# Long and short products in turn, with an accumulator of their own for the short ones

## The reference, cut to what matters

```python
x = x + rms_norm(concat(mixers(h @ w_in)) @ w_out)                      # first block
gate, val = split(conv(h @ ffn_up)); x = x + rms_norm((gelu(gate) * val) @ ffn_down)
x = x + 0.5 * (silu(h @ ffn1_w_gate) * (h @ ffn1_w_up)) @ ffn1_w_down # second block
y = attention(h @ w_in_2); x = x + gated(y @ w_dil_branch, y @ w_diff_branch) @ w_out_2
x = x + 0.5 * (silu(h @ ffn2_w_gate) * (h @ ffn2_w_up)) @ ffn2_w_down
```

## Time and profile before

| | |
|---|---|
| median of 3 runs | 3406.97 us (3406.35 to 3409.04) |
| the profiled execution | 3409.16 us |
| its span | 3407.3 us |
| TensorE matmuls busy | 3380.9 us, 99% |
| TensorE weight loads busy | 2953.4 us, 87% |
| VectorE / ScalarE / GpSimd busy | 2250.2 / 1746.8 / 541.1 us |
| DMA | 616.16 MB, 181 GB/s |

### The profile page before, as it was taken

One profiled execution on the slowest core, in us unless ns is written; L12 is line 12 of the kernel. 1 busy time (PEld: TensorE's weight loads), 2 busy tenths in 40 slices (PEclk: granted clock), 3 DMA queues, 4 the chain that ended last, 5 costly groups with the idle time before them and its releaser, 6 DMA issues.

```text
span 3407.3 us, 59138 instructions
## 1 busy us (share of the span) xinstructions
PE 3380.9 (99%) x19590; PEld 2953.4 (87%) x19590; DVE 2250.2 (66%) x2934; ACT 1746.8 (51%) x2591; POOL 541.1 (16%) x508
## 2 busy tenths in 40 slices
PE   9999999999999999999999999999999999999999
PEld 7898888888888888888888888888888888888888
DVE  7868687777754475555555599856687656556544
ACT  5445565555544455445444455544566544444433
POOL 1204111111100011111100056611100111111000
PEclk9999999999999999999999999999999999999999
DMA  6524545555566645555566655554556555555665
GB/s 210 161 94 147 189 152 185 190 190 186 188 187 190 189 157 187 185 191 189 186 184 191 215 173 177 181 167 157 171 192 196 188 188 186 187 192 186 185 192 171
DMA packets 175601, 616.16 MB, mean 181 GB/s; under 512 B 20864, under 2 KB 21408, under 8 KB 175136
## 3 DMA queue, kind: packets, MB, share of 16 engines
q1 hardware_dynamic: 175088, 609.84, 55.7%
q10 hardware_dynamic: 432, 5.24, 0.4%
HBM read 610.81 MB, written 4.19 MB: 180 GB/s over the span
## 4 chain that ended last, share of the span: by engine, by line
PE 95%; DVE 2%; issue 1%; ACT 1%; DMA 0%; POOL 0%; DVEq 0%; SPq 0%; POOLq 0%; ACTq 0%
PE acc L393 60%; PE acc L396 30%; DVE weights_low L279 1%; PE acc L408 1%; PE ps_scale L603 1%; PE ps_narrow L2297 0%; PE ps_wide L2273 0%; ACT weights_high L272 0%; PE acc L411 0%; DVE halves_memory L494 0%; PE ps_wide L1380 0%; PE ps_wide L1426 0%; PE ps_wide L1390 0%; PE ps_wide L1384 0%; DMA weights_raw<-in_w_diff_branch 0%
## 5 line engine op out<-in xcount | busy, mean ns | idle before, releaser
L393 PE MATMUL acc<-moving_halves,weights_high 128*128 128x512 f32 x6400 | 2039.6, 399 | 1.8 <-DVE x_T L2566 1.8
L279 DVE TENSOR_TENSOR weights_low<-weights_raw,weights_high 128x1024 fp32r<-128x1024 f32 (+2 forms) x1184 | 1450.0, 1237 | 738.0 <-ACT weights_high L272 736.7
L272 ACT ACTIVATE weights_high<-weights_raw 128x1024 fp32r<-128x1024 f32 (+2 forms) x1184 | 1220.6, 1032 | 797.5 <-PE acc L396 771.6
L396 PEld LDWEIGHTS acc<-moving_halves,weights_low 128*128 128x128 f32 x6400 | 1204.1, 188 | 284.2
L396 PE MATMUL acc<-moving_halves,weights_low 128*128 128x256 f32 x6400 | 1259.3, 278 | 0.0
L393 PEld LDWEIGHTS acc<-moving_halves,weights_high 128*128 128x128 f32 x6400 | 980.3, 189 | 13.3 <-issue 9.8
L393 PE MATMUL acc<-gated_halves,weights_high 128*128 128x512 f32 x2024 | 635.6, 395 | 0.0
L488 ACT ACTIVATE cross_products<-acc 128x256 f32<-128x256 f32 x509 | 194.6, 382 | 693.8 <-PE acc L396 693.7
L396 PEld LDWEIGHTS acc<-gated_halves,weights_low 128*128 128x128 f32 x2024 | 380.2, 188 | 89.9
L511 POOL TENSOR_TENSOR stage_scratch<-unscaled,token_scale 128x256 f32<-128x256 f32 x264 | 217.9, 826 | 1302.6 <-DVE unscaled L494 778.2
L396 PE MATMUL acc<-gated_halves,weights_low 128*128 128x256 f32 x2024 | 397.6, 278 | 0.0
(11 more groups left out here) (361 smaller groups left out, 1972.3 us busy)
## 6 DMA issues: line engine op xcount, KB each, us to landing
weights_raw<-in_w_in SPq DMA_DIRECT2D x271, 512.0 KB, 4.0
weights_raw<-in_ffn_up SPq DMA_DIRECT2D x176, 512.0 KB, 4.3
weights_raw<-in_ffn_w_gate SPq DMA_DIRECT2D x176, 512.0 KB, 4.1
weights_raw<-in_ffn_w_up SPq DMA_DIRECT2D x176, 512.0 KB, 4.6
weights_raw<-in_ffn_w_down SPq DMA_DIRECT2D x160, 512.0 KB, 3.9
weights_raw<-in_ffn_down SPq DMA_DIRECT2D x80, 512.0 KB, 4.2
weights_raw<-in_w_out SPq DMA_DIRECT2D x64, 512.0 KB, 3.8
weights_raw<-in_ffn_w_down SPq DMA_DIRECT2D x32, 256.0 KB, 2.7
```

The lines of the kernel that those rows point to most:

```text
L272: core.nc.scalar.activation(core.high[:, slot, k0:nk, :].rearrange("p a b -> p (a b)"), core.raw[:, slot, k0 * P:nk * P], ACT.Copy).then_i ...
L279: core.nc.vector.tensor_tensor(core.low[:, slot, k0:nk, :].rearrange("p a b -> p (a b)"), core.raw[:, slot, k0 * P:nk * P], core.high[:, s ...
L393: core.nc.tensor.matmul(acc[:, t % 2, :, :], core.high[:, u % SLOTS, k, :], parts[:, prod.first[t] + k0 + k, :, :], start=(k0 + k == 0), s ...
L396: core.last = core.nc.tensor.matmul(acc[:, t % 2, 0, :], core.low[:, u % SLOTS, k, :], parts[:, prod.first[t] + k0 + k, 0, :], start=False ...
```

## The change

A product can be marked with `place_apart`. Its short products then go to a second accumulator, the two banks of the first `ps_wide` tensor, and long and short matmuls are issued in turn: long, short, long, short. The take gets one more operation on VectorE: the short products' sum is added to `core.cross`, and the old addition waits for that. The products marked are `p_out`, `p_up`, `p_down`, `p_up1`, `p_down1`, `p_out2`, `p_up2` and `p_down2`; `p_in`, `p_in2` and `p_branch` keep the old form, and so do the joined last tiles. In the diff below, the counts for those tiles are left off by `last_joined`.

```diff
--- before.py
+++ after.py
@@ -79,6 +79,7 @@
         self.chunks = [(t, k0, min(KG, nk - k0)) for t, nk in enumerate(tiles) for k0 in range(0, nk, KG)]
         self.woven = woven
         self.halves = 0
+        self.apart = None
         self.per_body = len(self.chunks)
         assert not woven or tiles == [2 * KG, 2 * KG]
         assert self.per_body % SLOTS == 0 and len(tiles) % 2 == 0
@@ -92,6 +93,11 @@
         if scaled:
             core.scaled += self.bodies * len(self.tiles) - unscaled
         return self
+
+    def place_apart(self, core, last_joined=False):
+
+        self.apart, self.sum0 = core.second, core.sums
+        core.sums += self.bodies * len(self.tiles) - last_joined
 
     def of_body(self, i):
 
@@ -172,6 +178,8 @@
         self.slots_free = self.sem("slots_free")
         self.acc_free = self.sem("acc_free")
         self.cross_ready = self.sem("cross_ready")
+        self.apart_added = self.sem("apart_added")
+        self.sums = 0
         self.z_free = self.sem("z_free")
         self.y_scaled = self.sem("y_scaled")
         self.x_ready = self.sem("x_ready")
@@ -226,6 +234,8 @@
         self.wide = [self.ps(f"ps_wide{n}", [P, 8, P], ctx) for n in range(2)]
         self.narrow = self.ps("ps_narrow", [P, 4, P], ctx)
 
+        self.second = self.wide[0][:, :, :].rearrange("p (j h b) c -> p j h (b c)", j=2, b=2)
+
     def sem(self, name):
         return self.ctx.enter_context(self.nc.semaphore(name))
 
@@ -387,15 +397,25 @@
     _, _, nk = next(c for c in prod.chunks if c[0] == t and c[1] == k0)
     parts = core.h if prod.parts is None else prod.parts
     ks = range(pair, min(pair + 2, nk))
+    if prod.apart is None:
+        for k in ks:
+            if before is not None:
+                before(t, prod.first[t] + k0 + k)
+            core.nc.tensor.matmul(acc[:, t % 2, :, :], core.high[:, u % SLOTS, k, :],
+                                  parts[:, prod.first[t] + k0 + k, :, :], start=(k0 + k == 0), stop=False)
+        for k in ks:
+            core.last = core.nc.tensor.matmul(acc[:, t % 2, 0, :], core.low[:, u % SLOTS, k, :],
+                                              parts[:, prod.first[t] + k0 + k, 0, :],
+                                              start=False, stop=(k0 + k == prod.tiles[t] - 1))
+        return
     for k in ks:
         if before is not None:
             before(t, prod.first[t] + k0 + k)
+        ends = {"start": k0 + k == 0, "stop": k0 + k == prod.tiles[t] - 1}
         core.nc.tensor.matmul(acc[:, t % 2, :, :], core.high[:, u % SLOTS, k, :],
-                              parts[:, prod.first[t] + k0 + k, :, :], start=(k0 + k == 0), stop=False)
-    for k in ks:
-        core.last = core.nc.tensor.matmul(acc[:, t % 2, 0, :], core.low[:, u % SLOTS, k, :],
-                                          parts[:, prod.first[t] + k0 + k, 0, :],
-                                          start=False, stop=(k0 + k == prod.tiles[t] - 1))
+                              parts[:, prod.first[t] + k0 + k, :, :], **ends)
+        core.last = core.nc.tensor.matmul(prod.apart[:, t % 2, 0, :], core.low[:, u % SLOTS, k, :],
+                                          parts[:, prod.first[t] + k0 + k, 0, :], **ends)
 
 
 def multiply_joined(core, prod, acc, t, u, pair, k0, before):
@@ -491,6 +511,10 @@
 def take_tile(core, dve, prod, acc, out, i, t):
 
     dve.wait_ge(core.cross_ready, i * len(prod.tiles) + (prod.tile0 + t + 1))
+    if prod.apart is not None:
+        cross = core.cross[:, t % 2, :]
+        core.nc.vector.tensor_tensor(cross, prod.apart[:, t % 2, 0, :], cross, ALU.add).then_inc(core.apart_added, 1)
+        dve.wait_ge(core.apart_added, i * len(prod.tiles) + (prod.sum0 + t + 1))
     core.nc.vector.tensor_tensor(out, acc[:, t % 2, 0, :], core.cross[:, t % 2, :], ALU.add).then_inc(core.acc_free, 1)
 
 
@@ -2850,6 +2874,9 @@
 
         proj = Region(core.arena[:, :, :].rearrange("p k s -> p (k s)")).take(PROJ_TILES, PAD + S)
         core.accumulators(ctx)
+        for p, last_joined in ((p_out, True), (p_up, False), (p_down, True), (p_up1, False), (p_down1, False),
+                               (p_out2, False), (p_up2, False), (p_down2, True)):
+            p.place_apart(core, last_joined)
         begin = start_stage(core, p_in)
         mixers = Mixers(core, p_in, proj, mixed_parts)
         w_in = w_in_stage(core, p_in, mixers, lambda i, t: proj[:, 2 * i + t, PAD:PAD + S], p_out, proj[:, :, 0:PAD])
```

## The result

The changed kernel takes 3415.69 us, the median of 20 executions, against 3406.91 us before: a ratio of 1.0032, 95% interval 1.0023 to 1.0041. It is slower by 8.8 us, outside my own account's range of 3397 to 3412 (the whole range stated, 3350 to 3466, holds it), and it moved the other way than forecast. Its executions are not gathered round one time, as those before are (3405.4 to 3409.4). Sorted, 2 lie near 3400 us (3399.8 and 3399.9), 11 at 3413 to 3416 us and 7 at 3428 to 3429 us, in steps of 14 us.

What follows compares the result with a forecast made beforehand. TensorE's matmul stream, busy for 99% of the span, was taken to bound the kernel. From a 3407.3 us span, -3.4 us for order and +1.2 us for the take gave 3405.1, about 3405 us for the median; range 3350 to 3466 us.

Steps and rivals of the forecast that it cites:

- my own account: Whole kernel: order without weight, within the rounding; 3405 us, own range 3397 to 3412 us, chance 0.38.
- The order of the matmuls: TensorE's groups of four matmuls in the changed products: 0.6960 us in place of 0.697, -3.4 us give or take 7.
- The prediction's own sign of being wrong: TensorE's group length moves by over 2 ns, or TensorE waits for the take in the loops.
- The bank of the short products: Short products' second accumulator: a change of bank from short to long costs and gains nothing; long to short only bounded.
- The rival that it takes away a stall: Neighbours in one bank no longer stall TensorE: group falls to 0.680 us, 56 us less, 3352 us; chance 0.27.
- The added addition: VectorE's take, 0.58 us longer per tile: hidden except after three woven bodies and at one handover, together 1.2 us.
- The length rival: Each change of matmul length costs TensorE: group 0.7137 us, 56 us more, 3464 us; chance 0.27.
- VectorE late: The 0.58 us show on TensorE at each tile of the fullest product: 51 us more, 3456 us; chance 0.08.
- The bounds, 0.680 and 0.720 us: Ends for TensorE's group by pattern and place: -17 and +23 ns a group, -57 and +79 us on the kernel.
- the 216 ns: Long product's gap by the skill page's column formula; with 109 ns for short ones, 650 ns a group in either order.

Runs made afterwards that it cites:

- the moved kernel: The order-only kernel (long, short in turn, one bank, old take) with all operands 64 bytes further against the weights: 3436.92 us in a single execution.

## Why the prediction was wrong

- *The order of the matmuls, -3.4 us.* This is the step that failed. I took the group's length for one number, put together from the gaps of the old order. In the new order it has two, 0.6933 and 0.7067 us, on either side of my 0.6960, and each lasts through a whole product and the next. The term is -11 us where all products but `p_out` are short, and 28 us more than that where `p_up`, `p_down`, `p_up1` and `p_down1` are long. The prediction's own sign of being wrong, a group that moves by over 2 ns, came: 0.6967 us went to 0.6933 in some products and to 0.7067 in others.
- *The bank of the short products.* Right in its likeliest value: the bank alone leaves every product at its length of before, 0.6967 us, and 0.6933 in `p_out`. The rival that it takes away a stall was wrong.
- *The added addition.* Its price was right: 1.2 us forecast, 1.1 and 1.4 us measured in the old order against 3406.82 us of the kernel before, timed beside them, with TensorE's waits behind the woven bodies, as named. What I missed is that a wait of 0.3 us can do more than last 0.3 us. I summed the two terms as if they were free of each other, and the runs show that they are not: order -8 us, take +1 us, both together +19 us (3426.2 against 3406.9), a median of executions in three clusters.
- *The length rival, 0.7137 us in every product.* Wrong as a mechanism. It would have given one length and 56 us. The prediction gave "slower" its highest chance, 0.39, but through this rival, VectorE and rounding; that the kernel did get slower is no support for them.
- *VectorE late.* It went to 178.87 of 200 us in `p_up`, 89% (I had 86), and TensorE never waited for it in the loops. The 337 takes outside the first bodies of `p_up` and `p_up1` left the kernel within 1 us of the order alone.
- The bounds, 0.680 and 0.720 us, were real: the same columns run anywhere between them by pattern and by place, at 0.693, 0.697, 0.702 or 0.707 us as four matmuls and at 0.680, 0.707 or 0.720 us as six. The page of the Trainium skill named in the prediction, "TensorE: Matmul & The Clock Gate", section "Back-to-back issue gap", calls its formula by columns, from which the 216 ns come, the gap of a matmul in isolation; for a stream with weight loads it says that both set the spacing, and gives about 131 ns at 512 columns. The trace agrees with neither size: a long product took 0.23 to 0.24 us here.

What stays open is what the pattern is, and what in a wait chooses it. The times show that it lasts, that a wait can bring it in and a float32 matmul can end it, and that 64 bytes of the operand's place shift it. Two waits of the same length, 0.44 us, left different patterns, so the length of the wait alone does not choose.

## What to carry to other kernels

Where one engine's stream sets the time, read the period of its steady loop in every stage and not only the idle time: two loops with the same instructions and no gaps differed by 1.9% here, and the count of instructions in equal stretches showed it at once. A stall near the start of a long loop is to be weighed by the loop behind it, and a change is to be timed over many executions if its executions fall into steps. Try the place of an operand in memory before its order: 64 bytes gave 12 us in the old order, and with a single time. Measure it again with each order, since in the new one the same 64 bytes cost 38 us.

## What the runs showed of the hardware

- TensorE's stream of 512- and 256-column float32r matmuls with a weight load each has more than one lasting period at the same granted clock of 1.00. In turn it is 0.6933 or 0.7067 us a group, with long products at 0.23 or up to 0.24 us, and 0.702 us for the mixed halves of the moved kernel; as six matmuls of 256 columns 0.680, 0.707 or 0.720 us. In pairs each place of the operand showed only one, 0.6967 or 0.6933 us.
- GpSimd's scaling of the tiles (128x256) takes 1121 ns in place of 826 in the changed kernel, and 1123 ns in the kernel with the longer take alone, but 824 ns with the order alone. It isn't slower everywhere: in `p_up` it takes 0.75 to 0.85 us, no more than before, and about half of those in `p_up1` and `p_up2` take 1.7 us. The rows of `p_up1`, before and then changed, show what differs there. GpSimd began its operation 0.33 us ahead of VectorE's split of the weights before; the added operation moved it to 0.12 us behind the split's start, and now it ends 0.6 us after the split does. The split in turn went from 1.50 to 1.23 us. So the one that starts second of these two is held up. It cost nothing here, since GpSimd is idle for 82% of the span.

```profile
1405.13 0.75 POOL L511 TENSOR_TENSOR stage_scratch<-unscaled,token_scale 128x256 f32<-128x256 f32 x1 [5.13 <-DVE gated_halves L1138]
1405.46 1.50 DVE L279 TENSOR_TENSOR weights_low<-weights_raw,weights_high 128x1024 fp32r<-128x1024 f32 x1 [0.49 <-ACT weights_high L272]
```

```profile
1407.39 1.23 DVE L289 TENSOR_TENSOR weights_low<-weights_raw,weights_high 128x1024 fp32r<-128x1024 f32 x1
1407.51 1.72 POOL L535 TENSOR_TENSOR stage_scratch<-unscaled,token_scale 128x256 f32<-128x256 f32 x1 [5.20 <-DVE gated_halves L1162]
```
